# A third pair of up tiles without the seven-product scheme, an earlier reload, and two odd weight tiles projected at layer 0's end

## What is computed

```python
D_MODEL = 1024
SEQ = 1024
D_FF = 2816
def conv_ffn(h, w_in, conv_w, conv_b, w_out):
    u = h @ w_in
    C = u.shape[-1]
    u = lax.conv_general_dilated(u, conv_w[:, None, :], window_strides=(1,),
                                 padding=[(CONV_W - 1, 0)],
                                 dimension_numbers=('NWC', 'WIO', 'NWC'),
                                 feature_group_count=C) + conv_b
    gate, val = jnp.split(u, 2, axis=-1)
    return (jax.nn.gelu(gate, approximate=True) * val) @ w_out
...
for layer in range(DEPTH):
    g = norm_gains[layer]
    h = rmsnorm(x, g[0])
    ...
    x = x + rmsnorm(mix, g[1])
    h = rmsnorm(x, g[2])
    x = x + rmsnorm(conv_ffn(h, ffn_w_in[layer], ffn_conv_w[layer], ffn_conv_b[layer],
                             ffn_w_out[layer]), g[3])
return x
```

## Time and profile before

| | |
|---|---|
| median of 3 runs | 2566.87 us (2565.96 to 2571.13) |
| the profiled execution | 2568.79 us, of it the span of the trace 2567.0 us |
| TensorE busy | 2373.3 us, 92% of the span, 11619 matmuls |
| VectorE busy | 1671.2 us, 65% |
| ScalarE busy | 1189.6 us, 46% |
| GpSimd busy | 912.7 us, 36% |
| mean granted clock of TensorE | 0.964 |

### The profile page before, as it was taken

How to read it: one execution, slowest core, us unless ns; L and a number is a source line. 1 busy time by engine, 2 the same in 40 slices (tenths; PEclk the granted TensorE clock), 3 DMA queues, 4 the chain that set the end, 5 groups by cost and what they waited for, 6 DMA issues and landing times. The chain is left out here.

```text
span 2567.0 us, 31771 instructions
## 1 busy us (share of the span) xinstructions
PE 2373.3 (92%) x11619; PEld 1983.1 (77%) x11619; DVE 1671.2 (65%) x2408; ACT 1189.6 (46%) x1881; POOL 912.7 (36%) x670
## 2 busy tenths in 40 slices
PE   6889878989899899999999979899879999999998
PEld 5668667889777688888787867688767888887886
DVE  4564667865544788888636744556577888884365
ACT  4444777766533343443425532455423443443354
POOL 2101103401011688888200001132258888870000
PEclk9999988999999899999999989979989999999999
DMA  4001101000041122222664731221112222237475
GB/s 147 26 25 42 33 1 42 26 1 2 30 168 59 57 91 82 80 85 82 211 211 167 247 107 41 52 64 50 67 54 81 79 90 83 76 102 252 154 254 180
DMA packets 183156, 237.47 MB, mean 93 GB/s; under 512 B 14132, under 2 KB 135316, under 8 KB 183004
## 3 DMA queue, kind: packets, MB, share of 16 engines
...
## 5 line engine op out<-in xcount | busy, mean ns | idle before, releaser
L126 PE MATMUL l_ps<-l_t_hi,l_s_hi 128*128 128x512 f32 x480 | 186.7, 389 | 0.0
L126 PE MATMUL l_ps<-l_t_lo,l_s_hi 128*128 128x512 f32 x480 | 186.7, 389 | 0.0
L126 PE MATMUL l_ps<-l_t_hi,l_s_lo 128*128 128x512 f32 x480 | 186.7, 389 | 0.0
L2230 POOL TENSOR_TENSOR l_s_lo<-l_raw,l_s_hi 128x512 fp32r<-128x512 f32 x100 | 157.2, 1580 | 45.8 <-ACT l_s_hi L2134 45.8
L2230 POOL TENSOR_TENSOR l_s_lo<-l_w_sum,l_s_hi 128x512 fp32r<-128x512 f32 x80 | 168.6, 2128 | 6.1 <-ACT l_s_hi L2134 3.7
L2506 DVE TENSOR_TENSOR l_wlo<-l_raw,l_whi 128x1024 fp32r<-128x1024 f32 x68 | 83.2, 1223 | 101.2 <-ACT l_whi L2068 101.2
L194 POOL TENSOR_TENSOR wring_w_lo<-wring_raw,wring_w_hi 128x1024 fp32r<-128x1024 f32 x22 | 52.5, 2390 | 258.9 <-ACT wring_w_hi L190 258.9
L2068 ACT ACTIVATE l_whi<-l_raw 128x1024 fp32r<-128x1024 f32 x76 | 80.3, 1056 | 126.6 <-PE l_ps L126 118.9
L126 PE MATMUL l_ps<-odd_act_hi,l_s_hi 128*128 128x512 f32 x320 | 125.6, 392 | 11.5 <-POOL l_s_lo L2230 11.5
L126 PE MATMUL l_ps<-rest_hi,l_s_hi 128*128 128x512 f32 x320 | 125.6, 393 | 11.5 <-POOL l_s_lo L2230 11.5
L126 PE MATMUL l_ps<-rest_lo,l_s_hi 128*128 128x512 f32 x320 | 125.4, 392 | 0.0
...
## 6 DMA issues: line engine op xcount, KB each, us to landing
...
```

Source lines behind the costliest of these rows:

```text
L126: mm = pe.matmul(o, w, m, start=a, stop=z)
L2230: pool.tensor_tensor(s_lo[m % NW][:], weight_of(r, q), s_hi[m % NW][:].bitcast(F32), ALU.subtract).then_inc(s_lo_done, 1)
```

## The change

PLAIN becomes 3. Tiles 4 and 5 of the third pair are loaded, split and multiplied the plain way, into `ps[0]` and `ps[1]`; 19 pairs and 133 products are left. The first products wait for the taps of the last tile in their bank. The raw buffers swap their roles: the first pair of products loads behind the wait for the activations, the second where the up tiles' raw buffers were; the four `xsum` buffers move, GpSimd waits for the stores of x, and its `x_sums` alternate with `lo(3)` to `lo(5)`. In each round GpSimd makes the lo part of A11 before the sum for S2. VectorE's and ScalarE's queues at the start are written anew. Slots and bank waits of the first down tiles are computed from the last products.

SP issues load_gated(0) to (3) ahead of the store of gate 20; VectorE does `prepare(2)` ahead of the last taps.

At the end of layer 0 SP loads the first two odd weight tiles into `rawl` after w_lo of down tiles 62 and 63, ScalarE and GpSimd split them into two slots of the weight ring, and TensorE multiplies them with token half 0 into `ps[0]` and `ps[1]` after the last down tile; the transposes of blocks 6 and 7 stand inside the second, after k = 2 and k = 4. PSUM now lives across both layers, and in layer 1 projections 0 and 1 only do token half 1; SP begins there with weight tile 2, and ScalarE with hi(2), which waits for the first projection, then take(0), pack_keys, take(1), hi(3).

```diff
@@ -827,11 +831,11 @@
...
         wv = self.w.rearrange("(k p) c -> p k c", p=P)
-        for n in range(self.N_ALL):
-            if n >= 2:
-                sp.wait_ge(self.lo_done, n - 1)
+        for n in range(self.EARLY, self.N_ALL):
+            if n >= self.EARLY + 2:
+                sp.wait_ge(self.lo_done, n - 1 - self.EARLY)
             sp.dma_start(self.raw[n % 2][:], wv[:, :, self.COLUMN[n]:self.COLUMN[n] + P]).then_inc(self.w_in[n % 2], 16)
-            if n == 1:
+            if n == self.EARLY + 1:
                 sp.dma_start(self.sink[:].rearrange("p i s -> p (i s)"), self.sinks.partition_broadcast(P)).then_inc(self.sink_in, 16)
...
@@ -856,10 +860,9 @@
...
         def hi(n):
-            sc.wait_ge(self.w_in[n % 2], 16 * (n // 2 + 1))
-            if n >= 2:
-                sc.wait_ge(self.prod_done, n - 1)
-            sc.activation(self.w_hi[n % 2][:], self.raw[n % 2][:], ACT.Copy).then_inc(self.hi_done, 1)
+            sc.wait_ge(self.w_in[n % 2], 16 * ((n - self.EARLY) // 2 + 1))
+            sc.wait_ge(self.prod_done, n - 1)
+            sc.activation(self.w_hi[n][:], self.raw[n % 2][:], ACT.Copy).then_inc(self.hi_done, 1)
 
...
@@ -941,10 +944,8 @@
...
 
-        hi(0)
-        hi(1)
+        hi(2)
         take(N_KEY)
-        hi(2)
         pack_keys()
...
@@ -978,11 +979,9 @@
...
         pool.memset(self.v_odd[:, :, :, HD:VW], 1.0).then_inc(self.ones_set, 1)
-        for n in range(self.N_ALL):
-            pool.wait_ge(self.hi_done, n + 1)
-            if n >= 2:
-                pool.wait_ge(self.prod_done, n - 1)
-            pool.tensor_tensor(self.w_lo[n % 2][:], self.raw[n % 2][:], self.w_hi[n % 2][:].bitcast(F32), ALU.subtract).then_inc(self.lo_done, 1)
+        for n in range(self.EARLY, self.N_ALL):
+            pool.wait_ge(self.hi_done, n + 1 - self.EARLY)
+            pool.tensor_tensor(self.w_lo[n][:], self.raw[n % 2][:], self.w_hi[n][:].bitcast(F32), ALU.subtract).then_inc(self.lo_done, 1)
         for k in range(KT):
...
@@ -1036,12 +1035,14 @@
...
         def project(n):
-            pe.wait_ge(self.hi_done, n + 1)
-            if n >= 2:
+            left = slice(1, 2)
+            if n >= self.EARLY:
+                pe.wait_ge(self.hi_done, n + 1 - self.EARLY)
                 pe.wait_ge(self.taken, n - 1)
-            outs = [self.prod[n % 2][:, h] for h in H]
+                left = slice(0, 2)
+            outs, x_hi, x_lo = [self.prod[n % 2][:, h] for h in H][left], act.hi[left], act.lo[left]
             for k in range(KT):
-                hi_weight_passes(pe, outs, self.w_hi[n % 2][:, k, :], [x[:, k, :] for x in act.hi], [x[:, k, :] for x in act.lo], k == 0)
+                hi_weight_passes(pe, outs, self.w_hi[n][:, k, :], [x[:, k, :] for x in x_hi], [x[:, k, :] for x in x_lo], k == 0)
                 if k == 2 and n == N_KEY + 1:
...
@@ -1052,9 +1053,10 @@
...
                     rot(N_Q)
-            pe.wait_ge(self.lo_done, n + 1)
+            if n >= self.EARLY:
+                pe.wait_ge(self.lo_done, n + 1 - self.EARLY)
             for k in range(KT):
-                mm = lo_weight_pass(pe, outs, self.w_lo[n % 2][:, k, :], [x[:, k, :] for x in act.hi], k == KT - 1)
+                mm = lo_weight_pass(pe, outs, self.w_lo[n][:, k, :], [x[:, k, :] for x in x_hi], k == KT - 1)
             mm.then_inc(self.prod_done, 1)
...
     BLOCKS = ((0, 1, 2, 3), (4, 5), (6, 7))
-    PLAIN = 2
+    PLAIN = 3
     NT_UP = 2 * PLAIN
...
+    sums_of_x = [at(f"xsum{i}", [P, HALF], F32, G + a * KB) for i, a in enumerate((82, 84, 86, 76))]
     t4_sum = at("t4_sum", [P, QUARTER, HALF], F32, G + 68 * KB)
-    raw_pair = [None, {x: at(f"raw_{x}", [P, KT, P], F32, G + 48 * KB + 4 * KB * i) for i, x in enumerate("gv")}]
-    w_slots = [G + 56 * KB, G + 60 * KB] + [RING + 8 * KB * c + 4 * KB * i for c in (1, 2, 0) for i in range(2)]
-    NW = len(w_slots)
+    raw_pair = [{x: at(f"raw_{x}", [P, KT, P], F32, G + 48 * KB + 4 * KB * i) for i, x in enumerate("gv")}, None]
+    w_slots = [G + 56 * KB, G + 60 * KB] + [RING + 8 * KB * (c % 3) + 4 * KB * i for c in range(NT_UP - 3, NT_UP) for i in range(2)]
+    NW, NB = len(w_slots), 8
     s_hi = [at(f"s_hi{i}", [P, QUARTER, P], F32R, a) for i, a in enumerate(w_slots)]
...
@@ -1803,7 +1805,8 @@
...
     raw_up = [at(f"raw{i}", [P, KT, P], F32, RAW + 4 * KB * i) for i in range(2)]
-    raw_pair[0] = dict(zip("gv", raw_up))
+    raw_pair[1] = dict(zip("gv", raw_up))
+    raw_set = lambda r: (NS - 1 - r) % 2
     raw_far = {"m": [at(f"rawm{i}", [P, KT, P], F32, Y + 4 * KB * i) for i in range(2)],
...
+        last_in = lambda n, ring: n + (NP - 1 - n) // ring * ring
+        slot_free = sorted((max(last_in(2 + 2 * j + i, NW) for i in range(2)) + 1, (NT_UP + j) % 3) for j in range(3))
+        down_slot = lambda d: slot_free[d % 3][1]
         down_blocks = lambda d: BLOCKS[pass_of(d)]
+        if ahead:
+            next_in, next_hi, next_lo = [st.sem(f"next_in{i}") for i in range(2)], st.sem("next_hi"), st.sem("next_lo")
+            free_from = [NT_DOWN - 3 + i for i in range(2)]
+            next_raw, next_w = raw_far["l"], [[part[down_slot(d)] for d in free_from] for part in (whi, wlo)]
+
+
         down_cols = lambda d: slice(0, HALF) if d < FT else slice(0, 2 * P) if d < 2 * FT else slice(2 * P, HALF)
...
@@ -1920,15 +1934,15 @@
...
                 def load_pair(r):
-                    if r == 1:
-                        sp.wait_ge(t_sum, 4 * QUARTER)
-                    elif r >= 2:
+                    if r >= 2:
                         sp.wait_ge(s_lo_done, 7 * (r - 1))
+                    elif raw_set(r) == 0:
+                        wait_act(sp)
                     for j, x in enumerate("gv"):
-                        if r == 0:
+                        if r < 2 and raw_set(r) == 1:
                             sp.wait_ge(up_lo, NT_UP - 1 + j)
                         c = (off[x] + PLAIN + r) * P
-                        sp.dma_start(raw_pair[r % 2][x][:], wi[:, :, c:c + P]).then_inc(pair_in[r % 2], 16)
+                        sp.dma_start(raw_pair[raw_set(r)][x][:], wi[:, :, c:c + P]).then_inc(pair_in[raw_set(r)], 16)
 
...
@@ -1984,19 +1998,26 @@
...
                     mix_loads()
-                load_pair(0)
-                store_gated(0)
-                load_pair(1)
+                if raw_set(0) == 0:
+                    load_pair(0)
+                for u in range(4, NT_UP):
+                    load_up(u)
+                for r in range(1 - raw_set(0), 2):
+                    load_pair(r)
+                for i in range(PLAIN - 1):
+                    store_gated(i)
                 for r in range(2, NS):
                     load_pair(r)
-                    store_gated(r - 1)
+                    store_gated(PLAIN + r - 3)
                 load_down(0)
-                store_gated(NS - 1)
+                store_gated(FT - 3)
                 load_down(1)
...
                 load_down(3)
-                store_gated(NS)
-                for j in range(6):
+                for j in range(4):
+                    load_gated(j)
+                store_gated(FT - 2)
+                for j in range(4, 6):
                     load_gated(j)
...
@@ -2020,6 +2041,10 @@
...
                         load_x(TB + 7)
+                for i in range(2 if ahead else 0):
+                    w, columns = ahead
+                    wait_down_lo(sp, NT_DOWN - 4 + i)
+                    sp.dma_start(next_raw[i][:], w.rearrange("(k p) c -> p k c", p=P)[:, :, columns[i]:columns[i] + P]).then_inc(next_in[i], 16)
 
...
@@ -2143,14 +2168,22 @@
...
                 tap_last("v", 0)
+                split_w(4)
                 token_sums_hi(2)
+                tap_last("g", 1)
+                split_w(5)
+                gelu(1)
+                hi(0)
                 token_sums_hi(3)
-                tap_last("g", 1)
-                hi(0)
-                gelu(1)
-                for m in range(1, 6):
-                    hi(m)
                 tap_last("v", 1)
+                hi(1)
+                hi(2)
+                hi(3)
+                tap_last("g", 2)
+                hi(4)
+                gelu(2)
+                hi(5)
+                tap_last("v", 2)
                 hi(6)
...
@@ -2202,12 +2235,16 @@
...
                         split_h(TB + e - 3, ps[e - 7])
+                for i in range(2 if ahead else 0):
+                    sc.wait_ge(next_in[i], 16)
+                    wait_down_tile(sc, free_from[i])
+                    sc.activation(next_w[0][i][:], next_raw[i][:], ACT.Copy).then_inc(next_hi, 1)
                 first(TB + 6, ps[2])
...
                 second(TB + 7)
-                split_h(TB + 6, ps[0])
-                split_h(TB + 7, ps[1])
+                split_h(TB + 6, ps[2])
+                split_h(TB + 7, ps[3])
                 for i in range(2):
...
@@ -2234,20 +2271,26 @@
...
                 wait_act(pool)
-                x_sums(0)
-                lo(3)
```

(46 more changed lines are left out.)

65 lines of the change are left out of this document (36 added, 29 removed).

## The result

| | kernel before | changed kernel |
|---|---|---|
| median | 2569.00 us (2565.96 to 2572.81, 4 runs) | 2541.27 us (2540.12 to 2545.36, 4 runs) |
| profiled execution, its span | 2568.8, 2567.0 us | 2540.1, 2537.5 us |
| ratio, 95% interval | 1 | 0.989 (0.9875 to 0.9905) |
| TensorE busy, matmuls | 2373.3 us, 11619 | 2373.2 us, 11643 |
| mean granted clock | 0.964 | 0.969 |

The change takes 27.7 us by the medians and 29.5 us by the spans; 31.2 was forecast, 2537 against 2541.27. TensorE is busy as long as before with 24 matmuls more, so what was gained is idle time, and the better clock pays for the 24.

The account below looks back on a forecast made before the run. TensorE was taken to bound the kernel, with gains only where it stands still: 2 × 5.5 + 2.2 + 2.0 + 16.0 = 31.2 us off the profiled 2568.8 us gave 2537.6, stated as 2537. Range 2523 to 2552.

Parts of the forecast that it names:

- Part 1: Start of each layer's product loop: a third plain pair fills TensorE's wait; products end 5.5 us earlier per layer.
- what comes last: Ahead of product 0: VectorE's taps g2 finish last, so product 0 starts near 880.5 after a 3.2 us wait.
- the walk through VectorE's queue: Ahead of product 0: VectorE's sums, gate and taps timed one by one from 850.0 to taps g2 at 880.4.
- The half clock behind the wait: First products after TensorE's wait: the granted clock halves again, costing 2.5 us more.
- Rivals A: Ahead of product 0: VectorE less blocked, product 0 starts with tile 5's end; 5.7 us more per layer, 2526; chance 0.12.
- B: Ahead of product 0: VectorE's whole chain at blocked prices, product 0 at 887; 6.5 us worse per layer, 2550; chance 0.12.
- Part 2: Start of the down tiles: earlier gated reload leaves 1.7 us of waiting instead of 1.9 + 2.0; 2.2 us, 2.0 in layer 1.
- Part 3: Layer 0's end and layer 1's start: 48 projection matmuls fill the wait before the last transposes; 16.0 us gained.
- Both forecast waits: Layer 1's first projections: TensorE waits 0.8 us at `rot` and 2.3 us at turn_values(0).
- Rivals C: Layer 0's end pays little: half-clock matmuls delay the transposes 6.6 us, or TensorE restarts slow (3.1 us); 2546; chance 0.07.
- D: Start of the down tiles: reload not earlier because ScalarE or SP is late, both waits stay; 2541; chance counted in forecast.
- E: Product rounds: GpSimd's new order makes S2 later; with 1 us a round, 7 us of loss, 2575; chance 0.03.

Follow-up runs that it names:

- e2: Changed kernel with the store of gate 20 put back ahead of the gated reloads; 2538.86 us.
- e5: Changed kernel with ScalarE's order in layer 1 altered to take(0), hi(2), take(1) ahead of packing the keys; 2532.88 us.
- e8: Changed kernel with GpSimd's activation sums for k = 2 and 3 formed over 8 columns in place of 512; 2525.99 us.
- e4: Changed kernel with the work product 0 waits for put ahead of token sum 3, on VectorE and likewise ScalarE; 2533.21 us.
- e3: Kernel before with only the first four gated reloads put ahead of the store of gate 20; 2565.94 us.
- e7: Changed kernel with GpSimd's weight sum put back ahead of its split for each round's first product; 2544.35 us.
- e1: Changed kernel without its early projection: layer 0's end and the odd front as in the kernel before; 2560.24 us.

## Why the prediction was right, and where not

**What bounds the kernel, and Part 1's count of work: right.** TensorE without a hole in the products, 0.2267 us a matmul (1589 records in 359.85 us, 0.2265), 96 matmuls the plain way for 84 by products, 2.7 us more: all as forecast. Tiles 4 and 5 came without a wait.

**Part 1, what comes last: the mechanism right, its term a little small.** Product 0 does wait for taps g2, as the walk through VectorE's queue said, and half clock follows. The taps in order:

```profile
879.12 1.28 DVE L2482 SCALAR_TENSOR_TENSOR l_y_g<-trunk_ps,main_conv,l_y_g 128x1023 f32<-128x1023 f32 x1 [1.33 <-ACT l_y_g L2137]
880.44 1.28 DVE L2485 SCALAR_TENSOR_TENSOR l_y_g<-trunk_ps,main_conv,l_y_g 128x1022 f32<-128x1022 f32 x1
```

Forecast 880.5, which with the 0.7 us by which this trace runs late is 881.2; it was 881.87, since VectorE's chain ran 0.6 us behind the walk from token sum 2 on, whose inputs GpSimd gave at 851.36 (forecast 850.0 + 0.7). The wait was 5.34 us and not 3.2, mostly because the up tiles ended earlier than forecast (876.5, not 877.3 + 0.7): they ran at full clock behind the wait of 2.37 us, where the kernel before had half clock. That lengthens the wait but does not move product 0: in e2, with half clock there, it comes 60.2 us behind the first wide up half, in the changed kernel 60.0. The half clock behind the wait cost 363.8 − 361.8 = 2.0 us and not 2.5. So layer 0 gave its 5.4 us by two errors that cancel, 0.6 us too little for the chain and 0.5 too much for the clock.

Layer 1 gave 3.8 and not 5.5, product 0 being 1.7 us later than forecast (1921.74 against 1928.37 + 13.5 − 21.9 = 1920.0), and the half clock cost its 2.5 us. Of the 1.7 us some 0.7 are the chain again; 1.0 comes from a term that the forecast did not have. Behind the wait of 1.41 us ahead of the first wide up half the granted clock was half for longer than in e5, whose code is the same there, tile 0 ended later, and ScalarE's `tap_last("g", 0)` and all that stands behind it in the queues moved by 1.0 us. The windows from the first wide up half, then ScalarE's tap, first in the changed kernel (0.68 of the clock; the tap waits for TensorE and comes 8.20 us behind the start), then in e5 (0.82; no wait, 7.20 us). In layer 0, at full clock, it came 7.24 us behind:

```profile
1860.37:1868.57 8.20, 8.20 (x25) 6.57 (x26) 5.47 (x6) 1.87 (x3) 5.43 (x4) 0.68 0.65 192
...
1868.57 1.21 ACT L2137 ACTIVATE l_y_g<-trunk_ps,main_conv 128x1024 f32<-128x1024 f32 x1 [0.93 <-PE trunk_ps L126]
```

```profile
1855.11:1863.31 8.20, 8.20 (x30) 6.73 (x31) 5.46 (x6) 2.77 (x4) 5.45 (x4) 0.82 0.65 193
...
1862.31 1.19 ACT L2139 ACTIVATE l_y_g<-trunk_ps,main_conv 128x1024 f32<-128x1024 f32 x1
```

The term of the sum that was too small by 0.6 to 0.7 us is VectorE's chain up to taps g2. e8 shows that GpSimd beside it makes it so long, and e4 that only the order made product 0 pay for it. Rivals A (no wait) and B (7 us later) both fall.

**Part 2: the step that failed.** It took VectorE's place at the end of the rounds from the kernel before ("VectorE's merge starts at 1245.48 = T − 4.8") and carried it over. But Part 1 had made TensorE start 14.9 us later while VectorE's own chain moved by only 8.5 (the merge of the first round 887.03 to 895.51), so VectorE entered the rounds 6.4 us less behind and ended them with the merge at T − 10.3. Then both waits vanish, whatever SP does first: 4.2 + 3.9 us, where 2.2 + 2.0 were forecast. Of the 8.1 us the reload's order owns nothing; taken alone it is worth 2.4 and 1.0 us in e3. The bound given, 3.9 us a layer, was the two waits themselves; layer 1 gave just that and layer 0 0.3 more.

**Part 3: right in each place, 3 us too much by this pair of traces.** The 33 matmuls of projection hid the transposes' inputs (1508.08 without a wait), the weights were there, the transposes ran in 1.03 us at full clock, and the restart came at 1514.88, 1.2 us after VectorE's last operation ended. Both forecast waits came, 0.77 against 0.8 and 2.34 against 2.3 us. From the restart on, 128.6 us before became 120.1: 8.5 us, where 16.0 − 4.9 = 11.1 were forecast. The half clock behind the second wait was missed (from 1533.87 to that projection's end took 1544.61 − 1533.87 = 10.7 us, not 0.9 + 8.2 = 9.1, so 1.6 us), the projections ahead of it took 0.6 us more, and 0.4 us I can't place. Up to the restart the gain was 4.5 us and not 4.9, although the barrier took 0.7 us less than forecast. For 1.4 us of that belong to no edit: the down tiles behind the wait of 2.44 us ran at 0.83 of the clock here and at 1.00 in the kernel before.

```profile
1379.70:1389.70 10.00, 9.99 (x41) 8.18 (x42) 9.39 (x11) 3.91 (x7) 0.00 (x0) 0.83 0.62 184
```

```profile
1388.50:1398.50 10.00, 9.99 (x51) 8.21 (x52) 9.30 (x11) 4.72 (x8) 0.00 (x0) 1.00 0.62 202
```

Ten microseconds from the same matmul in each, the changed kernel first; up to the next transposes it took 7.17 us against 5.71. It varies from execution to execution: the same work, from T to the restart of layer 1, took 267.6 us in e4, 269.2 in the changed kernel, 269.8 in e5 and 272.3 in e7 (1516.63 − 1244.30). That limits every comparison of single traces here to some microseconds, unless a stretch is cut out that holds no such wait. It bears on Part 3 itself: e1 has the kernel before's code there, its down tiles ran at 0.96 of the clock where the kernel before's had 1.00, and against it Part 3 is worth 16.2 us, as forecast. So whether 16.0 was too much for the average execution stays open; the half clock behind the second wait was a term left out either way.

**Rivals C, D and E** fall by the rows above: C by the restart at 1514.88 and the transposes in 1.03 us, D by the reload issued at 1235.03 = T − 10.6 (the forecast had T − 10.9), E by e7.

**The sum.** −0.7 for the entry, −1.8 on Part 1, +3.9 on Part 2, −3.0 on Part 3: 31.2 becomes 29.6, and 29.5 was measured. The total owes its closeness to Part 2's miss lying against the other two, which is luck. The stated range, 2523 to 2552, is narrower than the bounds of the three parts added up, which give about 2519 to 2561; the measured 2541.27 lies inside both.
